# A gated-convolution layer in one block: transposing unnormed rows, applying the root later, and starting the output projection on early weight slices

## What is computed

```python
def rmsnorm(x, g):
    y = xf * lax.rsqrt(jnp.mean(xf * xf, axis=-1, keepdims=True) + RMS_EPS)
    return y * g
def short_conv_mixer(xn, prev, w_in, conv_k, w_out):     # xn = rmsnorm(h, norm_mix[0])
    c_gate, b_gate, hid = jnp.split(xn @ w_in, 3, axis=-1)
    u = c_gate * hid
    ucat = jnp.concatenate([prev, u], axis=1)
    conv = conv_k[0] * ucat[:, 0:s]
    for i in range(1, CONV_WIDTH):                       # CONV_WIDTH = 3
        conv = conv + conv_k[i] * ucat[:, i:i + s]
    y = (b_gate * conv) @ w_out
    return y, ucat[:, s:]
# forward: h = h + y, then the router, the experts, layer 1, final norm
```

## Time and profile before

| | us |
|---|---|
| median of 3 runs | 2475.37 (2472.98 to 2477.19) |
| the profiled execution, its own time | 2474.4 |
| its span, first to last instruction | 2471.8 |
| busy in the span: PE, DVE, ACT, POOL | 2225.1, 1301.4, 973.8, 408.0 |

### The profile page before, as it was taken

The page is one execution under the profiler, slowest core; times in us unless marked ns, Lnnn a source line. Parts: engine busy times, 40 slices in busy tenths (PEclk is TensorE's granted clock), DMA queues, the critical chain, the costliest instruction groups (busy, mean ns, idle before and its releaser), DMA issues. The chain is left out here.

```text
span 2471.8 us, 35253 instructions
## 1 busy us (share of the span) xinstructions
PE 2225.1 (90%) x12092; PEld 1944.9 (79%) x12093; DVE 1301.4 (53%) x1783; ACT 973.8 (39%) x1475; POOL 408.0 (17%) x246
## 2 busy tenths in 40 slices
PE   4999979879999998799999999996895999999980
PEld 4999967758888786588999999995685788888860
DVE  5365333355556854435555555453876445575545
ACT  4111122245555754221434444445233445475532
POOL 3444120010011000222222222213000000111003
PEclk8999989879999999799999999998896999999995
DMA  4111021257578966534244343437425476788556
GB/s 155 52 51 51 25 85 58 77 187 302 209 288 302 399 254 207 182 125 145 70 115 124 107 130 118 107 94 249 166 87 183 167 270 228 289 303 306 215 186 233
DMA packets 212200, 426.34 MB, mean 172 GB/s; under 512 B 34704, under 2 KB 87696, under 8 KB 208784
## 3 DMA queue, kind: packets, MB, share of 16 engines
q1 hardware_dynamic: 191344, 351.48, 41.2%
q0 software_dynamic: 12704, 46.14, 5.4%
q10 hardware_dynamic: 8064, 27.56, 2.8%
HBM read 350.15 MB, written 85.48 MB: 176 GB/s over the span
## 5 line engine op out<-in xcount | busy, mean ns | idle before, releaser
L1108 DVE TENSOR_TENSOR raw_low_w<-raw_w,raw_high_w 128x2048 fp32r<-128x2048 f32 x128 | 287.3, 2287 | 24.2 <-ACT raw_high_w L1034 21.8
L1711 PE MATMUL hd_pj<-lb_xh,lr_wh 128*128 128x384 f32 (+1 forms) x768 | 270.2, 352 | 5.5 <-PEq L1369 3.4
L1711 PE MATMUL hd_pj<-lb_xh,lr_wl 128*128 128x384 f32 (+1 forms) x768 | 252.1, 328 | 0.0
L1711 PE MATMUL hd_pj<-lb_xl,lr_wh 128*128 128x384 f32 (+1 forms) x768 | 252.0, 328 | 0.0
L1034 ACT ACTIVATE raw_high_w<-raw_w 128x2048 fp32r<-128x2048 f32 x120 | 223.1, 1912 | 20.1 <-DMA raw_w<-in_expert_w 20.0
L1108 DVE TENSOR_TENSOR e_wl_w<-raw_w,e_wh_w 128x2048 fp32r<-128x2048 f32 x64 | 143.8, 2289 | 159.8 <-ACT e_wh_w L1034 159.8
L341 PE MATMUL cv_pp<-lx_xh,lx_wh 128*128 128x384 f32 (+1 forms) x576 | 188.9, 328 | 2.3 <-POOLq L51 2.3
L341 PE MATMUL cv_pp<-lx_xl,lx_wh 128*128 128x384 f32 (+1 forms) x576 | 188.6, 327 | 0.0
L341 PE MATMUL cv_pp<-lx_xh,lx_wl 128*128 128x384 f32 (+1 forms) x576 | 188.6, 327 | 0.0
L971 PE MATMUL e_py<-e_wh_w,e_hh 128*128 128x512 f32 x416 | 170.5, 410 | 13.6 <-DVE e_hl L1122 8.9
L971 PE MATMUL e_pa<-raw_high_w,e_xh 128*128 128x512 f32 x416 | 168.2, 404 | 10.1 <-DVE e_xl L1118 5.1
(11 more groups left out here) (268 smaller groups left out, 4737.4 us busy)
## 6 DMA issues: line engine op xcount, KB each, us to landing
raw_w<-in_expert_w SPq DMA_DIRECT2D x96, 2048.0 KB, 12.1
s_ys<-e_ys ACTq DMA_DIRECT2D x52, 512.0 KB, 6.3
s_ys<-e_zero SPq DMA_DIRECT2D x32, 512.0 KB
lr_wr<-in_w_heads SPq DMA_DIRECT2D x32, 512.0 KB, 7.7
mg_og<-s_og SPq DMA_DIRECT2D x24, 520.0 KB, 5.2
h<-in_conv_w_in_t SPq DMA_DIRECT2D x7, 1536.0 KB, 6.5
s_og<-hd_ob SPq DMA_DIRECT2D x16, 520.0 KB, 6.3
hd_vb<-out_o_v SPq DMA_DIRECT2D x16, 512.0 KB, 7.4
```

Of the source, the lines that this page charges most:

```text
L1108: op = dve.tensor_tensor(wl[m][:, k, :], raw[m][:, k, :], wh[m][:, k, :].bitcast(F32), ALU.subtract)
L1711: mm = pe.matmul(pj[x % 2][:, 0:cn], w[:, q % 2, k, :], v[:, k, c0:c0 + cn], start=(k == 0 and m == 0), stop=(k == DK - 1 and m == 2))
```

## The change

The four blocks become one, `stage_conv`, with no barrier between its parts.

- The rows are loaded tile by tile and transposed as they come, without the norm. The first three tiles are transposed ahead of the products, the other six inside chunk 0, one after each half part (12 products). The first weight slice is loaded on ACT's queue.
- The norm's scale is applied later. DVE builds diagonals of the inverse of the mean square; PE spreads them over the partitions by products with a matrix of ones (`spread`, nine 128-column products inside chunk 1), ACT copies them to `r2row`, and DVE multiplies C by them. The root itself is applied in `finish`, to the projected rows.
- The gain is applied by ACT and DVE while they split the weights, now in eight pieces of 384 columns a slice. POOL has no work in the convolution.
- The taps run chunk by chunk, directly after each chunk's `u`.
- Two slices of the output weights (`EARLY`) are split during the last convolution slice, together with the first tile of `zT`. The projection begins on them; the other six (`LATE`) follow, one of them split by POOL and five by DVE. The input rows come back in two steps with a semaphore each.

```diff
-            for u in range(TILES // 3):
-                full = min(u * 3 + 3, QT)
-                sp.dma_start(G.h[:, u * 3:full, :], x[:, u * 3:full, :]).then_inc(W.x_ready[u], 16)
+            for t in range(QT):
+                sp.dma_start(G.h[:, t, :], x[:, t, :]).then_inc(x_ready[t], 16)
...
+            act.dma_start(G.gcol[:, :, :], A["gains_col"]).then_inc(c_ready, 16)
+            act.dma_start(first, A["conv_w_in_t"][0]).then_inc(first_ready, 16)
...
+            def x_transposes(t):
+                pe.wait_ge(x_ready[t], 16)
+                if t >= 3:
+                    pe.wait_ge(xl_ok, t)
...
+                    for part in range(3):
+                        for half in range(2):
+                            mm = products(f, n, part, range(half * DK // 2, (half + 1) * DK // 2))
...
+                            if m == 0:
+                                x_transposes(3 + 2 * part + half)
+                        if m == 1:
+                            spread(part)
...
+            def w_low(f):
+                for k in range(DK):
+                    dve.wait_ge(wh_ok, f * DK + k + 1)
+                    dve.scalar_tensor_tensor(out=flat(cwl[f % 2][:, k]), in0=flat(weight(f)[:, k]), scalar=gain(k),
+                                             in1=flat(cwh[f % 2][:, k]).bitcast(F32), op0=ALU.mult, op1=ALU.subtract).then_inc(wl_ok, 1)
...
-            pool.tensor_tensor(flat, flat, g, ALU.mult).then_inc(scaled, 1)
-            pool.wait_ge(high_ok, f + ONE)
-            pool.tensor_tensor(wl[:, u], raw[u], wh[:, u].bitcast(F32), ALU.subtract).then_inc(low_ok, 1)
+            for n, k in enumerate(POOL_LOW):     # POOL_LOW = (2,)
+                pool.wait_ge(out_high, HIGH[k])
+                pool.tensor_tensor(M.wl[k][:, :], out_raw[k], M.wh[k][:, :].bitcast(F32), ALU.subtract).then_inc(out_low[1], 1)
...
+                link(dve.tensor_tensor(csb[:, v, 0:cn], pair[0][:, v, 0:cn], r2row[:, c0:c0 + cn], ALU.mult))
...
+            KS = EARLY + LATE                    # (0, 1) + (2, 3, 4, 7, 5, 6)
+            pe.wait_ge(zl_ok, 1)
+            pe.wait_ge(r2_ok, NC)
+            pe.wait_ge(*out_low_of(EARLY[-1]))
+            for half in range(2):
+                project(0, half, EARLY)
+            for k in LATE:
+                pe.wait_ge(*out_low_of(k))
+                for half in range(2):
+                    project(0, half, (k,))
...
+            for k in (2, 4):
+                sp.wait_ge(*out_low_of(k))
+            sp.dma_start(G.h[:, 0:3, :], x[:, 0:3, :]).then_inc(again[0], 16)
...
+                add = dve.scalar_tensor_tensor(out=row, in0=product, scalar=scale, in1=row, op0=ALU.mult, op1=ALU.add)
```

More of the change, by code:

```diff
@@ new lines, in _ @@
+            act.wait_ge(filled, 1)
+            act.activation(M.warm[:, :], G.ssq[:, TILES - 1:TILES], ACT.Square)
+            for t in range(3):
+                x_high(t)
+            w_high(0)
+            for t in range(3, TILES):
+                x_high(t)
+                square(t - 3)
+            for t in range(TILES - 3, TILES):
+                square(t)
+            gate_copy(0, 0)
+            inverse_row(0)
+            w_high(1)
+            inverse_row(1)
+            inverse_row(2)
@@ new lines, in _ @@
+            for k in LATE:
+                if k == 5:
+                    act.wait_ge(z_ok, DK * NC)
+                out_high_part(k)
+            z_high(1)
+            z_high(2)
+            for n in range(TILES):
+                if n + 3 < TILES:
+                    z_high(n + 3)
+                lower(n)
+                if n < TILES - 1:
+                    F.square(act, n, added)
+                    F.root(act, n)
+                    for part in range(2):
+                        F.copy(act, n, part)
@@ new lines, in _ @@
+            for k in DVE_LOW[len(EARLY):]:
+                out_low_part(k)
+            z_low(1)
+            z_low(2)
+            dve.wait_ge(root_ok, 1)
+            dve.wait_ge(again[0], 16)
+            for n in range(TILES - 1):
+                if n == 3:
+                    dve.wait_ge(again[1], 32)
+                finish(n)
+                if n + 3 < TILES:
+                    z_low(n + 3)
+                F.variance(dve, n)
+                F.inverse(dve, n)
+                F.normed(dve, n)
+                if n >= 1:
+                    F.bias(dve, n - 1)
@@ L420, in stage_conv @@
+            n = TILES - 1
+            finish(n)
+            F.bias(dve, n - 1)
+            F.copy_last(dve)
+            F.variance(dve, n)
+            F.inverse(dve, n)
+            F.bias(dve, n)
+            dve.wait_ge(late, 32)
     c.close()
@@ new lines, in layer_conv @@
+    M.close()
+    cx = Ctx(nc, "lx_")
+    M.cwh = [cx.sb(f"wh{u}", [P, DK, 3, P], F32R) for u in range(2)]
+    M.csb = cx.sb("csb", [P, 2, 384])
+    M.acc = cx.sb("acc", [P, NTOK])
+    M.kc = cx.sb("kc", [P, DK, CONV])
+    M.hist = cx.sb("hist", [P, DK, DEC_B, CONV - 1])
+    cx.sb("gap", [P, DK * D - cx.used])
+    M.cwl = [cx.sb(f"wl{u}", [P, DK, 3, P], F32R) for u in range(2)]
+    M.xh = cx.sb("xh", [P, DK, NTOK], F32R)
+    M.xl = cx.sb("xl", [P, DK, NTOK], F32R)
+    assert cx.used >= top
```

764 lines of the change are left out of this document (341 added, 423 removed).

## The result

| | before | after |
|---|---|---|
| median | 2474.7 us (2472.98 to 2477.19) | 2432.93 us (2429.75 to 2435.42) |
| the profiled execution, its own time | 2474.4 | 2429.75 |
| its span | 2471.8 | 2428.0 |
| busy: PE, DVE, ACT, POOL | 2225.1, 1301.4, 973.8, 408.0 | 2214.1, 1283.8, 975.2, 300.6 |

Four runs of each, in turn on one chip: ratio 0.983, 95% interval 0.981 to 0.984. The changed kernel is 1.7% faster; 2433.0 was predicted.

What follows compares the result with a forecast made beforehand. PE was taken as bound by its products in the convolution and idle at the start and hand-over. -34.3 + 8.6 + 3.6 + 0 - 20.2 = -42.3 us from 2474.4 gave 2432.1, median 2433 us; range 2420 to 2447.

Steps and rivals of the forecast that it cites:

- Step 1: Start of the kernel: three tiles transposed as they land, first product at 15.3 instead of 49.6, 34.3 us earlier.
- Step 2: Chunk 0: six tiles transposed inside it, 7.0 us, plus 1.6 us of stalls; 8.6 us later.
- Step 3: Chunk 1: nine 128-column float32 spread products at 0.4 us each; 3.6 us later.
- Step 4: Convolution chunks: same products, DVE needs 15 of the 35.4 us a slice, nothing becomes late; 0 us.
- Step 5: Hand-over to the projection: tile 1's second half 21.5 us after the last convolution product; 20.2 earlier including the former low clock.
- the low clock there before: Hand-over: PE's products ran at the low clock for about 3 us in the kernel before; 1.6 us more gained.
- A: Rival, hand-over: the clock falls in PE's gaps and all 30 late products are slow; +6 us, 2439; chance 0.14.
- B: Rival, start: gains or third tile land late and chunk 0 stays at low clock; +4 and +8, 2445 together; chance 0.12.
- D: Rival, early chunks: PE isn't kept fed, chunk 2 waits for the first `u`; 2439 us; chance 0.05.
- C: Rival, convolution: DVE becomes the bound, 42 us a slice against PE's 35.4; 54 us lost, 2487; chance 0.02.

Runs made afterwards that it cites:

- rows_first: Changed kernel with the first weight slice issued behind the third row tile on SP's queue and transposes waiting for the identity alone; 2432.34 us.
- after_again: The changed kernel itself, unchanged, measured again in five runs on another chip; 2431.01 us, ratio 0.980 to the kernel before.
- norm_first: Changed kernel with each row tile normed before its transposes, no spread and no late root; 2429.86 us, repeated as norm_first_again with five runs, 2432.13 us.
- taps_by_slice: Changed kernel with taps and gate run once over the whole last slice, so the first tile of zT is split only after them; 2441.30 us.
- rows_in_threes: Changed kernel with the rows loaded in transfers of three tiles again instead of tile by tile; 2436.05 us.

## Why the prediction was right

The two places named, the start and the hand-over, are where the time was won, and the loop between them stayed bound by its products. The time was met to 0.1 us, which is luck: errors of 1 to 3 us cancel, and executions of one kernel differ by more. Step by step, by the marks of the profiled executions (PE's first product of chunk 1 as the end of chunk 0, 64.63 before; the 65.01 of the earlier trace rows is ACT's copy):

| step | predicted | measured |
|---|---|---|
| 1. first product | -34.3 | -33.6 |
| 2. chunk 0 | +8.6 | +6.8 |
| 3. spread, and 4. chunks | +3.6 | +2.5 |
| 5. hand-over, to the second half of tile 1 | -18.6 | -19.8 |
| the low clock there before | -1.6 | -1.1 |
| behind it, up to the router | 0 | -1.6 |
| behind the router | 0 | +3.0 |
| the span | -42.3 | -43.8 |

**Step 1** was right in size and half wrong in its reason. The gains landed at 6.2, not 7.2, but the third tile held PE until 11.0, and its transposes took 1.97 us: 13.0 instead of 12.7. What I had named as a lesser bound, the third tile beside the weight slice, was one of two causes, as rows_first showed. The prediction put the start of the kernel before down to the norm's chain. The chain was there, but some 8 us of it were DVE standing still beside POOL (4.52 and 5.22 us, above), which the sum took away without naming it.

**Step 2** was over-costed by 1.8 us. The stalls were as counted (1.8 us against 1.6). About 1 us lies in the tiles: the first took 1.03 us and not 1.8 (in after_again 1.59, so that part is chance), and the last, of 64 rows, 0.68. Another 1 us is the low clock that I carried over: the products ran 0.32 us apart for 3.2 us here (15.96 to 19.2), against 5.4 us before, at 0.15 us a product.

**Step 3** was over-costed by about 1 us: the 18 records take 2.6 us, 0.15 each, and removing them in norm_first shortened the 23 chunks by 2.4. I had preferred a row taken after an idle time; the transposed piece of the same width (0.13 in the earlier trace rows) was the better neighbour, at two records a product.

```profile
42.10 0.83 PE L240 MATMUL cv_tp<-lc_zT,ones 128*128 128x128 f32 x6
...
46.97 0.83 PE L240 MATMUL cv_tp<-lc_zT,ones 128*128 128x128 f32 x6
...
51.83 0.97 PE L240 MATMUL cv_tp<-lc_zT,ones 128*128 128x128 f32 x6
```

**Step 4** held: from 43 to 312.3 PE never waits, with DVE busy for 115 of 269 us.

**Step 5** followed the forecast operation by operation: POOL's slice at 4.2 after the last product (4.9 forecast), the gate's end at 6.4 (7.0), slice 3 at 7.7 (8.6), tile 1's second half at 20.4 (21.5). The experiments give its parts, which overlap: without taps by chunk the transposes come 11.4 later, without early slices 6.5, with slice 2 on DVE 0.8 earlier.

**Behind the mixer** I had set nothing. Up to the router 1.6 us more were gained: before, the clock had fallen when the last logits were made, and after the change it fell behind them. The same 16 small products, before and after:

```profile
479.44 3.60 PE L480 MATMUL po_pl<-po_wr,po_xt 128*128 128x20 f32 x16
```

```profile
434.02 2.23 PE L607 MATMUL cv_pp<-po_wr,po_xt 128*128 128x20 f32 x16 [0.25 <-ACT po_xt L625]
```

Then 3.0 us were given back; what stayed were 0.8 and 1.5 at the two gathers of the experts' rows and 0.8 at the last expert's hidden part. The second gather and the last wait, before the change and after it:

```profile
1902.86 1.54 PE L978 MATMUL e_tp<-ident,e_xg 128*128 128x128 f32 x6 [8.08 <-POOLq L952]
...
2405.83 0.76 PE L971 MATMUL e_py<-e_wh_w,e_hh 128*128 128x512 f32 x1 [8.93 <-DVE e_hl L1122]
```

```profile
1858.38 1.97 PE L947 MATMUL e_tp<-ident,e_xg 128*128 128x128 f32 x8 [9.62 <-POOLq L921]
...
2362.03 0.76 PE L940 MATMUL e_py<-e_wh_w,e_hh 128*128 128x512 f32 x1 [9.77 <-DVE e_hl L1091]
```

The last wait goes up and down by execution: it was 8.9 in norm_first, norm_first_again and taps_by_slice and 9.7 to 9.8 in the other nine, at the same code. So does the first gather, 9.8 to 10.7 against 9.87. The second gather does not: it took 9.6 to 10.5 in all twelve executions after the change, against 8.08 in the one trace before. Whether the change lengthened it was not tried.

**The rivals.** A is real, but not at the price I gave: the clock fell in four of eight such hand-overs and cost 1.6 us each time, not 6. I had priced all 30 late products as slow; the rows of after_again show some 4 us at the low clock. Of B only the third tile's 1.1 us of wait came, and PE's rate was up by 19.2; D did not happen, chunk 2 never waited. C is refuted twice: with POOL idle the taps cost 510 ns for at most 384 columns, and with POOL made busy for 54 us PE still lost nothing.

## What to carry to other kernels

When an engine waits at the seam of two stages, ask first what can be handled in smaller pieces across the seam, and only then what can be left out or done later: here 24 us were won at the start, and the rearranged arithmetic of the norm had at most 2 of them. Look also for a third engine that stops one of the chain while it works: at the start of the kernel before, that was some 8 us by estimate, and it stands in the length of DVE's operations, while the waits of PE name DVE alone. Two things that feed the same product (weight slices and `zT`) have to come early together; with one of them late PE still waited 7.6 or 12.7 us. Compare variants by marks just behind the place that was changed, since a few microseconds won there disappear among those that the rest of the program loses and gains from one execution to the next.

## What the runs showed that was not expected

- A kernel has two lengths of the same hand-over, 20.1 and 21.7 us, with the same gaps of PE in both; which one comes differs between executions of the same code (332.26 and 333.89 minus the last product at 312.17 and 312.19).
- PE's first products after the start came 0.32 us apart for 3.2 us, and 0.17 after it, while the granted clock of that stretch reads 1.00 (15.90:22.00 above). In after_again, the same code, the same low rate stands beside a clock of 0.50 (columns as in the earlier trace rows). So the column can miss the low clock of the start in one execution and have it in another; the distance of the products shows it in both.

```profile
15.05:18.40 3.35, 3.35 (x11) 3.35 (x12) 3.35 (x7) 2.11 (x5) 0.00 (x0) 0.50 1.04 356
```

- The 12 KB of gains landed 4.9 to 5.4 us after their issue in the executions with rows of 512 KB a transfer on the other queue, and 6.7 us in rows_in_threes (6.0 before the change) beside transfers of 1.5 MB. The identity, 64 KB and issued just ahead on the same queue, went the other way: 4.0 to 4.4 us beside the 512 KB, 3.1 and 1.8 beside the 1.5 MB. A small constant that the first instruction needs can be late by several us; the size of its neighbours alone doesn't say which one.
